# Recurrence order, row halves, and attention scores inside the last recurrent round, with GpSimd scaling the rows

## The chip, the cores and the metric

The kernel runs on one core of one Trainium2 chip. The metric is the device time of one execution in microseconds; the runs of the kernel before gave 2823.59 to 2827.82 us with a median of 2827.42. The engines of the core are TensorE (matrix products, with its weight loads), VectorE, ScalarE, GpSimd and SyncE, which issues transfers.

## The reference

Two transformer blocks on 256 positions of width 2048, in float32. The first block is normed, projected by w_in, and its columns are shared between two mixers. Then follow an output projection, a cross attention to a memory, and an MLP; the second block is a gated chunk mixer and a convolutional feed-forward with modulation from `ada_w`. The change lies in the two mixers of the first block.

The first mixer is a recurrence over 16 heads of 64 (RWKV-7):

```python
w = -jax.nn.softplus(-(w0 + jnp.tanh(xw) @ w_decay_up)) - 0.5
decay = jnp.exp(-jnp.exp(w.astype(f32)))
a = jax.nn.sigmoid(a0 + xa @ a_up)
g = jax.nn.sigmoid(xg) @ g_up
kk = heads(k * k_k); kk = kk / jnp.maximum(jnp.sqrt(jnp.sum(kk * kk, axis=-1, keepdims=True)), 1e-12)
k = k * (1.0 + (a - 1.0) * k_a)
def step(state, inp):
    r_t, w_t, k_t, v_t, kk_t, a_t = inp
    sa = jnp.einsum('bhvk,bhk->bhv', state, -kk_t)
    state = (state * w_t[:, :, None, :] + sa[..., None] * (kk_t * a_t)[:, :, None, :]
             + v_t[..., None] * k_t[:, :, None, :])
    return state, jnp.einsum('bhvk,bhk->bhv', state, r_t)
# ... y is normed per head, (yn + bonus) * g, bonus = sum(r k r_k) v
```

The second mixer is sparse attention with 8 query heads and 2 key heads of 128. An index score (16 heads of 64, relu, weighted sum) picks 64 of the causal keys for each query; the kernel turns the choice into a bias of 0 or -1e30 and does an ordinary softmax:

```python
s = jnp.einsum('bqhgd,bqkhd->bqhgk', qg, kg) * (ATT_HEAD ** -0.5)
prob = jax.nn.softmax(jnp.where(valid, s, -inf), axis=-1)
o = jnp.einsum('bqhgk,bqkhd->bqhgd', prob, vg)
```

## The kernel before, in words

The sequence is 256 positions (T), kept as two blocks (b = 0, 1) of 128 rows or four chunks of 64 columns. Each engine's instructions are written out in one order by hand; an engine does them in that order. Waits are on counters: `Steps` gives each step of a list a name, `done` counts it up when the instruction ends, and `wait(engine, lane, round, name)` makes the engine wait until that step has been counted. The lists (PD, PA, PT for the preparation, CD, CA, CT for the core of the recurrence, YD, YA, YT for its tail, HD, HA, HT for the attention, the last letter for VectorE, ScalarE or TensorE) must hold the steps in the order in which they are done.

**Recurrence.** It is done in four rounds (i = 0 to 3) of two lanes (g = 0, 1), each lane a tile of two heads. Within a chunk the recurrence is the inverse of a triangular matrix, found by doubling: for level lv = 1 to 5 TensorE multiplies (`product`, step p), ScalarE copies the product out of PSUM (c), TensorE squares and multiplies (`doubled`, step q), and VectorE merges the results by a masked copy into `xx` (x for one half, z for the other; line 787). Then TensorE applies the inverse (`applied`: au, ry, mn), VectorE forms the carried sums (`state`: r2 on line 795, mt, nn on line 804, st on line 809, with the products s1 and s2 of line 1101 in between) and TensorE the outputs (yy, line 1109). The tail norms them (`mean`, `variance`, `inverse`, `normed`, `low_part`).

The tiles of round i + 1 are prepared between the levels of round i. On TensorE: the head norms (line 930) and the decay and gain LoRA products (`lora_t`, lines 939 and 940) ahead of the first doubling, the gate (lines 947 and 948) ahead of the second, the spread norm (line 953) ahead of the third, the bonus product (`bonus_t`, line 968) ahead of the fifth. The LoRA weights of decay and gain have 64 rows each that are not zero. On VectorE: norm km after level 1, inverse after 2, key after 3, decay sum and bonus input bp after 4, bonus bo (line 740) and the decayed tiles of both lanes (`decayed_d`: at on line 747, b0 on line 750, bk on line 751, rt on line 753) after 5, ahead of `state`. TensorE turns the decayed tiles (`turn_t`, lines 979 to 983): lane 0 between s1 and s2, lane 1 after yy. In the last round nothing is prepared.

**Attention.** The index scores (`index_tensor`, line 625) and the choice of keys are made within the projection; the bias is ready at 288 us. At the end of the last round TensorE makes the score products of heads 0 to 3 (line 1137). After `low_part(3)` VectorE takes for head k the score out of PSUM with scale and bias (sm, line 903), two row maxima (ma, mb) and their negative (ng); ScalarE does the exponentials with row sums (line 458); VectorE takes the reciprocal (rc) and scales the rows (na, nb, lines 912 and 913); TensorE turns the three 128x128 squares (line 1148), ScalarE copies them (pc, line 465), TensorE multiplies with the values (lines 1205 to 1207) and makes the scores of head k + 4, and the result is split in a high part (h, line 470) and a low part (lo, line 917). Four tiles `sm` serve eight heads in turn. All engines wait for the last HD step before the output projection; SyncE fetches its first four blocks and ScalarE the memory tensor when the recurrence's tail is done. GpSimd has nothing to do from 288 us to 538 us.

## Time and profile before

| what | value |
|---|---|
| median of 3 runs | 2827.42 us |
| profiled execution, its own time | 2827.2 us |
| span | 2825.4 us |
| instructions | 49020 |
| TensorE busy | 2725.5 us (96%) |
| VectorE busy | 2024.3 us (72%) |
| ScalarE busy | 1395.1 us (49%) |
| GpSimd busy | 173.7 us (6%) |
| mean granted TensorE clock | 0.981 |
| recurrence, first chunk product to last low part | 333.14 to 500.70 us |
| attention, to its last low part | 500.70 to 523.28 us |

The span is the time from the first to the last instruction of the profiled execution. Busy times count an engine's instructions, not its waits. Matrix products are pipelined, so a busy TensorE is not one at its peak. The granted clock is a share of 2.4 GHz: 1.00 is 2.4 GHz and 0.50 is 1.2 GHz. A float32 product shows as two records. In the timelines a row is a run of alike instructions: its start, its length, the engine, the line and the tiles (written<-read), how many, and in brackets the idle time before it and what ended that.

### The profile page before, as it was taken

What the parts mean: (1) busy time and instruction counts of PE and PEld (TensorE: products, weight loads), DVE (VectorE), ACT (ScalarE), POOL (GpSimd) and SP (SyncE); (2) the same over time, 40 slices, a digit from 0 to 9 for tenths busy, and PEclk for the clock granted to TensorE, in tenths of its full rate; (3) what the DMA queues carried; (4) which work ended last, traced back from release to release, by engine and by line L of the source; (5) the groups of instructions that cost most, each with busy time, mean ns of one, the idle gap of its engine ahead of it and who ended that gap; (6) DMA issues with size and microseconds to landing.
All of it is one profiled execution on the core that took longest, in us unless ns stands there. A gap on an engine that the chain in (4) does not pass through costs nothing.

```text
span 2825.4 us, 49020 instructions
## 1 busy us (share of the span) xinstructions
PE 2725.5 (96%) x17934; PEld 2335.7 (83%) x17934; DVE 2024.3 (72%) x3189; ACT 1395.1 (49%) x2215; POOL 173.7 (6%) x211
## 2 busy tenths in 40 slices
PE   9999988799899999999999999999999999999997
PEld 8877777687688888888876888888878888888886
DVE  5566566686788887878888766668787656775675
ACT  5444454555544444444445454445465545554554
POOL 4500000210100000000030000000100000000002
PEclk9999999899999999999999999999999999999999
DMA  6554200454477777887767865567745555555553
GB/s 213 173 170 153 98 3 3 160 176 149 163 284 281 276 285 263 292 292 269 276 238 264 295 243 167 180 239 283 260 157 185 191 190 186 181 190 187 181 186 135
DMA packets 157712, 573.35 MB, mean 203 GB/s; under 512 B 17984, under 2 KB 18272, under 8 KB 157120
## 3 DMA queue, kind: packets, MB, share of 16 engines
q1 hardware_dynamic: 154368, 562.11, 58.0%
q10 hardware_dynamic: 2064, 7.50, 0.7%
q8 instruction: 141, 2.31, 0.3%
q0 software_dynamic: 1072, 0.89, 0.2%
q14 instruction: 67, 0.55, 0.1%
HBM read 567.57 MB, written 2.10 MB: 202 GB/s over the span
## 4 chain that ended last, share of the span: by engine, by line
PE 84%; DVE 9%; POOL 3%; issue 2%; ACT 2%; DMA 0%; POOLq 0%; DVEq 0%; ACTq 0%
PE ps L2298 45%; PE ps L2299 24%; DVE wlo L1978 3%; PE ps L2301 3%; PE ps L2323 2%; PE ps L2325 2%; PE ps L2324 2%; DVE tt L2063 1%; POOL tab L288 1%; PE ps L1646 1%; DVE tt L2005 1%; POOL ssm L1734 0%; PE ps L1035 0%; ACT whi L1755 0%; DVE xn L2052 0%
## 5 line engine op out<-in xcount | busy, mean ns | idle before, releaser
L1978 DVE TENSOR_TENSOR wlo<-raw,whi 128x1024 fp32r<-128x1024 f32 x872 | 1061.5, 1230 | 399.2 <-ACT whi L1755 397.7
L2298 PE MATMUL ps<-xn,whi 128*128 128x512 f32 x3540 | 1261.8, 401 | 12.5 <-issue 5.1
L1755 ACT ACTIVATE whi<-raw 128x1024 fp32r<-128x1024 f32 x872 | 907.1, 1054 | 586.1 <-PE ps L2299 516.9
L2299 PE MATMUL ps<-xn,wlo 128*128 128x256 f32 x3776 | 1053.6, 282 | 0.0
L2298 PE MATMUL ps<-act_in,whi 128*128 128x512 f32 x2444 | 871.5, 401 | 7.5 <-issue 3.4
L2298 PEld LDWEIGHTS ps<-xn,whi 128*128 128x128 f32 x3540 | 669.3, 189 | 178.7 <-issue 11.0
L2299 PE MATMUL ps<-act_in,wlo 128*128 128x256 f32 x2624 | 732.0, 282 | 0.0
L2299 PEld LDWEIGHTS ps<-xn,wlo 128*128 128x128 f32 x3776 | 717.6, 190 | 5.1
L2298 PEld LDWEIGHTS ps<-act_in,whi 128*128 128x128 f32 x2444 | 462.5, 189 | 122.1 <-DVE wlo L1978 4.8
L2299 PEld LDWEIGHTS ps<-act_in,wlo 128*128 128x128 f32 x2624 | 498.8, 190 | 4.0
L1762 ACT ACTIVATE hl<-ps 128x256 f32<-128x256 f32 x416 | 155.4, 375 | 354.9 <-PE ps L2301 354.9
L2005 DVE TENSOR_TENSOR tt<-ps,hl 128x256 f32<-128x256 f32 x272 | 113.6, 418 | 161.0 <-ACT hl L1762 159.3
L1732 POOL COPY ss<-tt 128x256 f32<-128x256 f32 x5 | 2.6, 527 | 1955.2 <-ACT tt L1793 1955.2
L1804 ACT ACTIVATE act_in<-tt 128x256 fp32r<-128x256 f32 x140 | 56.6, 418 | 123.7 <-DVE tt L2160 88.7
L2323 PE MATMUL ps<-whi,xn 128*128 128x512 f32 x288 | 112.6, 391 | 3.8 <-issue 1.8
L2325 PE MATMUL ps<-whi,xn 128*128 128x512 f32 x288 | 112.2, 389 | 0.0
L2324 PE MATMUL ps<-wlo,xn 128*128 128x512 f32 x288 | 112.1, 389 | 0.0
L1998 DVE SCALAR_TENSOR_TENSOR ada<-adaq,silu_c,ada 128x512 f32<-128x512 f32 (+1 forms) x128 | 100.5, 785 | 2.3
L1998 DVE SCALAR_TENSOR_TENSOR ada<-adaw,silu_c,ada 128x512 f32<-128x512 f32 (+1 forms) x112 | 83.9, 749 | 2.4
L2301 PE MATMUL ps<-xn,whi 128*128 128x512 f32 x236 | 85.0, 394 | 0.0
L1734 POOL TENSOR_TENSOR ss<-ss,tt 128x256 f32<-128x256 f32 x75 | 67.7, 903 | 217.5 <-ACT tt L1793 214.5
L2005 DVE TENSOR_TENSOR zc<-ps,hl 128x256 f32<-128x256 f32 x88 | 37.0, 420 | 56.0 <-ACT hl L1762 56.0
(329 smaller groups left out, 2095.5 us busy)
## 6 DMA issues: line engine op xcount, KB each, us to landing
raw<-in_stream SPq DMA_DIRECT2D x872, 512.0 KB, 4.2
adaw<-in_ada SPq DMA_DIRECT2D x96, 512.0 KB, 5.6
adaq<-in_ada SPq DMA_DIRECT2D x96, 512.0 KB, 4.9
h<-in_xT SPq DMA_DIRECT2D x4, 512.0 KB, 7.6
memx<-in_memT ACTq DMA_DIRECT2D x1, 2048.0 KB, 9.3
out<-fin SPq DMA_DIRECT2D x4, 512.0 KB, 2.6
lwa<-in_lora ACTq DMA_DIRECT2D x1, 1536.0 KB, 8.2
wst<-in_wsT ACTq DMA_DIRECT2D x1, 1024.0 KB, 4.8
```

What stands on the lines that cost most here:

```text
L1734: pool.tensor_tensor(acc[:, :], acc[:, :], new, ALU.add).then_inc(ss_done, 1)
L1755: act.activation(whi[:, r, :], raw[:, r, :], ACT.Copy).then_inc(hi_done, 1)
L1762: act.activation(hl[:, t, :], ps[:, lin.bank(g, t), T:2 * T], ACT.Copy).then_inc(hl_done, 1)
L1978: dve.tensor_tensor(wlo[:, r, :], raw[:, r, :], whi[:, r, :].bitcast(F32), ALU.subtract)\
L1998: ins = dve.scalar_tensor_tensor(dst, w, s, dst, ALU.mult, ALU.add)
L2005: dve.tensor_tensor(dst, ps[:, lin.bank(g, t), 0:T], hl[:, t, :], ALU.add).then_inc(evac_done, 1)
L2298: pe.matmul(ps[:, b, :], whi[:, r, w], x[:, kc, :], start=first, stop=False)
L2299: ins = pe.matmul(ps[:, b, 0:T], wlo[:, r, w], x[:, kc, 0:T], start=False, stop=False)
L2301: ins = pe.matmul(ps[:, b, :], whi[:, r, w], x[:, kc, :], start=False, stop=True)
L2323: pe.matmul(out, hi, whi[:, r, w], start=first, stop=False)
L2324: pe.matmul(out, hi, wlo[:, r, w], start=False, stop=False)
L2325: ins = pe.matmul(out, lo, whi[:, r, w], start=False, stop=last)
```

## The change

1. VectorE's masked copies of a level do x of both lanes first and then z of both (before: x and z of lane 0, then of lane 1).
2. The bonus product of the next round stands after the last doubling on TensorE, not before it.
3. `decayed_d` is split in two (at and b0; `grown_d`: bk and rt). Lane 0's stay ahead of `state`; lane 1's stand inside it, the first half ahead of s2 and the second ahead of s3.
4. The LoRA products read only the 64 rows of their part, and each part has its own bank (decay in one, gain in the other, the lanes side by side); ScalarE reads them there. In the index scores the loops over heads and blocks are swapped, so that products of the upper and the lower 64 rows alternate.
5. In the last round the scores of heads 0 to 3 are made behind the doublings of levels 1 to 4, VectorE does their maxima behind its copies of these levels, and ScalarE their exponentials ahead of its copies for levels 3, 4 and 5 and ahead of `applied`. At the end of the round TensorE makes the scores of heads 4 to 7, and in the attention none.
6. There are eight tiles `sm`. GpSimd scales the rows, each head after its reciprocal. VectorE's loop is reciprocal k, maxima k + 4, low part k - 2; ScalarE's is exponentials k + 4, copy k, high part k - 1.

```diff
@@ level copies, bonus product, decays
         def doubled(i, lv):
-            for g in lanes:
-                CT.wait(dve, g, i, f"q{lv}")
-                for w in range(2) if lv < 5 else (1,):
+            for w in range(2) if lv < 5 else (1,):
+                for g in lanes:
+                    if w == 0 or lv == 5:
+                        CT.wait(dve, g, i, f"q{lv}")
...
             product(i, 5)
+            doubled(i, 5)
             if more:
                 bonus_t(pe, i + 1)
-            doubled(i, 5)
             applied(i)
...
             for c in (1, 2):
+                if i < 3:
+                    (decayed_d, grown_d)[c - 1](dve, i + 1, (1,))
                 for g in lanes:
...
                 bonus_v_d(dve, i + 1)
-                decayed_d(dve, i + 1)
+                decayed_d(dve, i + 1, (0,))
+                grown_d(dve, i + 1, (0,))
             state(i)
@@ row halves
+        for g in lanes:
+            n, o = 2 * i + g, slice(g * T, (g + 1) * T)
+            for k in range(2):
+                r = rows(k)
+                ins = pe.matmul(bank(i, k, "wa")[:, o], lwa(n, k)[r, :], lora_in(0)[r, :], start=True, stop=True)
+            PT.done(ins, g, "wa")
...
-            for hd in range(2):
-                q = slice(CH * hd, CH * hd + CH)
-                for b in range(2):
+            for b in range(2):
+                for hd in range(2):
+                    q = slice(CH * hd, CH * hd + CH)
@@ last round: TensorE (lv 1 to 4), ScalarE (k = 0 to 3), VectorE (k = 0 to 3)
             doubled(i, 1)
+            if not more:
+                scores(0)
             product(i, 2)
...
                 root_k_a(act, i + 1)
+            else:
+                exponentials(0)
             product(i, 3)
...
                 norm_k_d(dve, i + 1)
+            else:
+                JP.wait(dve, 0, 0, "d1")
+                maxima(0)
             doubled(i, 2)
...
                 if i < 3:
                     PD.wait(pe, g, i + 1, "bo")
+                else:
+                    HD.wait(pe, 0, 0, f"sm{2 + g}")
@@ attention: GpSimd, then VectorE
+        for k in range(8):
+            HD.wait(pool, 0, 0, f"rc{k}")
+            for b, name in enumerate("ab"):
+                v = sm[k][:, 0:P] if b == 0 else sm[k][:, P:384]
+                HP.done(pool.tensor_scalar(v, v, sx_[:, k, 2 + b:3 + b], None, ALU.mult), 0, f"n{name}{k}")
...
+        for k in range(10):
             if k < 8:
+                HA.wait(dve, 0, 0, f"eb{k}")
+                hd_(f"rc{k}", dve.reciprocal(sx_[:, k, 2:4], sx_[:, k, 2:4]))
+            if k < 4:
+                maxima(k + 4)
+            if k >= 2:
+                q = k - 2
                 HA.wait(dve, 0, 0, f"h{q}")
...
         def turned_p(k):
-            HD.wait(pe, 0, 0, f"nb{k}")
+            HP.wait(pe, 0, 0, f"nb{k}")
```

## Rows read from the trace of the kernel before

**Rows 1.** The page's chain that ended last: shares of the span by engine.
```profile
PE 84%; DVE 9%; POOL 3%; issue 2%; ACT 2%; DMA 0%; POOLq 0%; DVEq 0%; ACTq 0%
```

**Rows 2.** Windows: stretch, busy by engine (records), TensorE clock, DMA share, GB/s.
```profile
333.14:500.70 167.56, 142.84 (x3669) 121.34 (x3668) 103.91 (x314) 77.12 (x182) 0.00 (x0) 0.94 0.04 12
500.70:523.28 22.58, 14.66 (x88) 12.40 (x88) 18.30 (x65) 15.66 (x50) 0.00 (x0) 0.77 0.47 186
411.00:420.00 9.00, 7.96 (x64) 6.66 (x66) 3.21 (x13) 3.36 (x8) 0.00 (x0) 0.62 0.01 2
447.00:450.00 3.00, 3.00 (x47) 3.00 (x48) 1.44 (x4) 0.00 (x0) 0.00 (x0) 0.52 0.02 5
```

**Rows 3.** Chain of waits, second round: start us, us, what ran.
```profile
402.63 0.49 DVE bp L734
405.44 0.64 DVE bo L740 x2
409.68 0.67 DVE r L795 x2
411.68 0.48 DVE nn L804 x2
```

**Rows 4.** Timeline of VectorE, first and third round, between the state products.
```profile
373.75 0.48 DVE L809 SCALAR_TENSOR_TENSOR st<-ps,e,nn 128x64 f32<-128x64 f32 x2 [1.00 <-PE ps L1101]
...
458.72 0.50 DVE L809 SCALAR_TENSOR_TENSOR st<-ps,e,nn 128x64 f32<-128x64 f32 x2 [1.85 <-PE ps L1101]
```

**Rows 5.** Timeline of VectorE, last round: levels, then state.
```profile
473.30 1.44 DVE L787 COPY_PREDICATED xx<-mk,ps 128x256 f32<-128x256 int32 x4 [0.34 <-PE ps L1049]
475.74 1.43 DVE L787 COPY_PREDICATED xx<-mk,ps 128x256 f32<-128x256 int32 x4 [1.00 <-PE ps L1049]
...
480.59 0.44 DVE L787 COPY_PREDICATED xx<-mk,ps 128x256 f32<-128x256 int32 x1 [0.94 <-PE ps L1049]
...
487.31 0.66 DVE L804 TENSOR_SCALAR nn<-ps,e 128x64 f32<-128x64 f32 x3
```

**Rows 6.** Timeline of TensorE: LoRA products of two rounds, then one index score.
```profile
343.69 0.91 PE L939 MATMUL ps<-proj,lwa 128*128 128x256 f32 x2 [1.40 <-DMA lwa<-in_lora]
...
427.97 0.68 PE L939 MATMUL ps<-proj,lwa 128*128 128x256 f32 x2
...
429.35 0.59 PE L940 MATMUL ps<-proj,lwa 128*128 128x256 f32 x2
...
125.08 0.93 PE L625 MATMUL ps<-ki,proj 64*128 64x128 f32 x8
```

**Rows 7.** Line 625 alone, from 125.10 to 125.11: records running then.
```profile
L625 PE MATMUL ps<-ki,proj x2: 373/373/373, 125.1 to 125.1; 64*128 64x128 f32 x2
```

**Rows 8.** Timeline of VectorE in the attention: first two heads, then the end.
```profile
500.62 0.55 DVE L903 SCALAR_TENSOR_TENSOR sm<-ps,bias 128x384 f32<-128x384 f32 x1
501.93 0.55 DVE L903 SCALAR_TENSOR_TENSOR sm<-ps,bias 128x384 f32<-128x384 f32 x1
...
519.93 0.34 DVE L913 TENSOR_SCALAR sm<-sm,sx__211 128x256 f32<-128x256 f32 x1
...
522.85 0.42 DVE L917 TENSOR_TENSOR act_in<-ps,act_in 128x256 fp32r<-128x256 f32 x1 [0.42 <-ACT act_in L470]
```

**Rows 9.** Timeline of TensorE: the attention's first product.
```profile
504.40 0.90 PE L1148 MATMUL ps<-ident,sm 128*128 128x128 f32 x3 [7.44 <-DVE sm L913]
```

**Rows 10.** Timeline of GpSimd in the projection: two products of a table by a constant.
```profile
61.73 1.92 POOL L288 TENSOR_SCALAR tab<-tp 128x256 f32<-128x256 f32 x1
...
97.61 0.85 POOL L288 TENSOR_SCALAR tab<-tp 128x256 f32<-128x256 f32 x1
```

**Rows 11.** Timeline of VectorE beside the first of these.
```profile
61.71 1.23 DVE L1978 TENSOR_TENSOR wlo<-raw,whi 128x1024 fp32r<-128x1024 f32 x1 [1.61 <-ACT whi L1755]
```

**Rows 12.** Timeline of ScalarE after the attention: a table load and its activation.
```profile
567.26 1.28 ACT L1773 ACT_TABLE_LOAD   x1
568.87 0.42 ACT L1773 ACTIVATE nx<-nx 128x256 f32<-128x256 f32 x1 [0.32 <-DVE nx L2029]
```

More of the change, by code:

```diff
@@ L418, in high, with exponentials @@
                 YA.done(act.activation(act_in[:, 2 * i + g, 0:T], yq[g][:, :], ACT.Copy), g, "hi")
+        def exponentials(k):
+            HD.wait(act, 0, 0, f"ng{k}")
+            for b in range(2):
+                v = sm[k][:, 0:P] if b == 0 else sm[k][:, P:384]
+                HA.done(act.activation(v, v, ACT.Exp, bias=sx_[:, k, b:b + 1], accum_out=sx_[:, k, 2 + b:3 + b]),
+                        0, f"e{'ab'[b]}{k}")
         unit(0)
@@ L441, in scalar @@
                 decays_a(act, i + 1)
+            else:
+                exponentials(3)
             applied(i)
@@ L740, in bonus_v_d, with decayed_d @@
             pd(dve, i, g, "bo", dve.tensor_tensor(bo[2 * (i % 2) + g][:, :], bank(i, g, "bs")[:, 0:T], tiles(2 * i + g)[2], ALU.mult))
-    def decayed_d(dve, i):
-        for g in lanes:
+    def decayed_d(dve, i, which=lanes):
+        for g in which:
             q = 2 * (i % 2) + g
@@ L749, in decayed_d, with grown_d @@
             pd(dve, i, g, "at", ins)
-            pd(dve, i, g, "b0", dve.tensor_tensor(tb[i][g][:, 0, :], kk[i][g][:, :], aa[i][g][:, :], ALU.mult), True)
+            pd(dve, i, g, "b0", dve.tensor_tensor(tb[i][g][:, 0, :], kk[i][g][:, :], aa[i][g][:, :], ALU.mult))
+    def grown_d(dve, i, which=lanes):
+        for g in which:
+            q = 2 * (i % 2) + g
+            PD.wait(dve, g, i, "b0")
             pd(dve, i, g, "bk", dve.tensor_tensor(bk[q][:, :, :], tb[i][g][:, :, :], e2[i][g][:, :].unsqueeze(1).to_broadcast([P, 2, T]),
@@ L851, in low_part, with hd_, maxima @@
                                                   ALU.subtract))
+        def hd_(name, ins, chain=False):
+            HD.done(ins, 0, name)
+            if chain:
+                HD.wait(dve, 0, 0, name)
+        def maxima(k):
+            HT.wait(dve, 0, 0, f"s{k}")
+            hd_(f"sm{k}", dve.scalar_tensor_tensor(sm[k][:, :], ps[:, (2, 6, 3, 7)[k % 4], 0:384], ATT_SCALE, bias[:, :],
+                                                   ALU.mult, ALU.add), True)
+            hd_(f"ma{k}", dve.tensor_reduce(sx_[:, k, 0:1], sm[k][:, 0:P], AX_X, ALU.max))
+            hd_(f"mb{k}", dve.tensor_reduce(sx_[:, k, 1:2], sm[k][:, P:384], AX_X, ALU.max), True)
+            hd_(f"ng{k}", dve.tensor_scalar(sx_[:, k, 0:2], sx_[:, k, 0:2], -1.0, None, ALU.mult))
         for g in lanes:
@@ L865, in vector @@
                 inverse_k_d(dve, i + 1)
+            else:
+                maxima(1)
             doubled(i, 3)
@@ L868, in vector @@
                 key_d(dve, i + 1)
+            else:
+                maxima(2)
             doubled(i, 4)
@@ L872, in vector @@
                 bonus_d(dve, i + 1)
+            else:
+                maxima(3)
             doubled(i, 5)
@@ L966, in bonus_t @@
             PD.wait(pe, g, i, "bp")
-            PA.wait(pe, g, i, "aa")
+            for z in lanes:
+                PA.wait(pe, z, i, "aa")
             PT.done(pe.matmul(bank(i, g, "bs")[:, 0:T], blk[:, 0, :], bp[i][g][:, :], start=True, stop=True), g, "bs")
@@ L1131, in scores @@
             if k < 2:
[L1132 to L1135 removed]
+                CA.wait(pe, k, 3, "zw")
+            elif k < 4:
+                YD.wait(pe, k - 2, 2, "yn")
+            else:
+                CA.wait(pe, k % 2, 3, "y1")
+                CD.wait(pe, k % 2, 3, "n2")
             for b in range(2):
@@ L1168, in tensor @@
             doubled(i, 2)
+            if not more:
+                scores(1)
             product(i, 3)
@@ L1172, in tensor @@
             doubled(i, 3)
+            if not more:
+                scores(2)
             product(i, 4)
             doubled(i, 4)
+            if not more:
+                scores(3)
             product(i, 5)
+            doubled(i, 5)
             if more:
                 bonus_t(pe, i + 1)
-            doubled(i, 5)
             applied(i)
@@ L1182, in tensor @@
             else:
-                for k in range(4):
+                for k in range(4, 8):
                     scores(k)
```

91 lines of the change are left out of this document (29 added, 62 removed).

## The prediction

> **What bounds the kernel now.** I read the chain of waits first, then the windows by stage, then the timelines of the engines in the stages that the change touches. TensorE holds 84% of the chain that ended last [rows 1], and nearly all of that lies in the weight streams, which the change leaves alone. What it touches is the recurrence (333.14 to 500.70 us, 167.6 us) and the attention behind it (500.70 to 523.28 us, 22.6 us) [rows 2]. No engine is full there: TensorE is busy 142.8 us of the first and 14.7 of the second, VectorE 103.9 and 18.3. The work goes back and forth between the engines in small pieces, so an order that lets a piece start earlier moves the end. In the attention VectorE, 81% busy, is closest to a bound. The stage behind starts when all attention steps are counted, so what is won or lost here moves the rest of the program as a whole. The four weight blocks and the memory tensor, 4.2 MB, land within the attention (186 GB/s over 22.58 us [rows 2]); in 19 us they would need 220, which the page's slices show to be common (up to 295), so they stay hidden.
>
> **The change part by part.** Everything is set against the profiled execution, 2827.2 us with a span of 2825.4; that is 0.2 us below the median of the runs, so the difference carries over. A time within 0.2% (5.7 us) of it is what a measurement can't tell from no change.
>
> *Bonus product behind the last doubling, and lane 1's decays later.* In the second round the bonus input bp is ready at 403.12 us. Then came bonus product, doubling, x5 and bo (up to 406.08), 3.6 us of decays for two lanes, the state's first sum at 409.68, and the three products nn of lane 1, done at 412.16 [rows 3]: 9.0 us. With the new order the last doubling is done while VectorE still makes bp, and x5 follows bp at once. From there the path is what the last round shows, where VectorE has no decays to make: from the end of lane 0's x5 (481.03) to the end of nn (487.97) [rows 5], 6.94 us. Add 0.44 for that x5 and 0.22 for the later end of VectorE's copies (below): 7.6 us, 1.4 saved. VectorE's bo and lane 0's decays (0.7 + 1.8 us) fit beside TensorE's and ScalarE's steps, with 0.3 to spare. This counts in three rounds: -4.2. In the third TensorE was granted 0.52 of its clock (the 1.2 GHz level) from 447 to 450 us [rows 2], inside this path, and the new order has the idle time before it cut by the doubling; half of the 1.4 us that this costs, -0.6, is counted. Bounds: 0 to -2.5 a round.
>
> *Where lane 1's decays go.* They now stand between the state products: 0.86 us ahead of s2 and 1.0 ahead of s3, in front of both lanes' steps. In the first round VectorE sat idle there for 1.00 us, in the third for 1.85 [rows 4], since TensorE's transposes, at 1.2 GHz in the second and third round, took longer. So 1.86 us don't fit in the first (+0.9) and do in the two others (0). If TensorE keeps its clock in those two, it is +0.9 each, but then the transposes and chunk products win more.
>
> *Order of the copies.* x of both lanes, then z of both. The second x must wait for lane 1's doubling, so VectorE ends about 0.2 us later, and lane 1's next product starts up to 0.15 earlier. Where VectorE goes on to something urgent (km before the gate product, bp) it costs 0.2; elsewhere nothing. The 0.2 is in the sums here.
>
> *Row halves.* The LoRA products run over 64 rows each, decay on the upper and gain on the lower half, into two banks. Before, four 128-row products took from 427.97 to 429.9 us [rows 6], about 0.46 each, on TensorE's path. If halves run side by side two pairs take 0.9: 0.9 saved, less 0.2 for another tile shape and 0.2 for km: -0.5 a round. That different tiles do run together the index scores show: 10 ns after their first record started, two are running [rows 7]. In the first round these products run slower (0.91 for the first pair of records against 0.68 [rows 6]): -1.1. The product pair in the projection, where TensorE is the bound: -0.5. Together -2.6, bounds 0 and -4.4. The Trainium skill ("TensorEngine Tiling (Array Packing)", Key Properties) says that a change of tiling mode drains the engine; by it each LoRA block pays a drain on both sides, where before it paid one, and this is a rule against the edit. No row has this very switch. In the index scores the same edit is only a swap of loops: as two records already run together, it brings 0; if those two are halves of one product, 0.2 x 8 = -1.6 at most, kept for the range.
>
> *Last round: scores and maxima inside.* Four score products (384 columns each; the index score of as many took 0.93 us [rows 6]) lie beside VectorE's copies and cost nothing. VectorE's maxima of one head take 1.31 us (500.62 to 501.93 [rows 8]) and stand in front of the next level's copies. Its idle time there is 1.00 us a level [rows 5]. So VectorE becomes the bound: free at 472.96, level 2 starts at 474.27 instead of 473.30; each further level is 1.36 + 1.31 = 2.67 instead of 2.44; x5 starts at 482.28 instead of 480.59: +1.7. The exponentials lie in ScalarE's idle time (it is busy 77 of 168 us [rows 2]). They need a table load of 1.28 us, but a load ran ahead of the wait of its activation (567.26, the activation then still waited 0.32 [rows 12]), so it lies beside VectorE's work. The Sqrt table comes back after the state and is hidden by the scores of heads 4 to 7. If the load is not hidden it is +1; low bound +0.8, high +3.
>
> *Attention.* VectorE loses four maxima (5.2 us) and all scalings (0.34 us for the larger half of a head [rows 8]); GpSimd gets the scalings. A 128x256 product by one constant took it 0.85 us [rows 10]; for 128x128 I take 0.5, with the gap 1.45 a head (bounds 1.3 and 3.0). Nothing can start before VectorE has the last low part and the first reciprocal, so heads 0 to 3 still pass GpSimd one after the other. First head, in us from the start: reciprocal 0.3, GpSimd done at 1.8, transposes 0.9 ([rows 9]: TensorE is at its lower clock after the idle time, as before) to 2.8, copy 3.3, next head's transposes, product to 5.5, high part 6.0, low part 6.45. VectorE's order puts the reciprocal of head 3 behind that low part, and the one of head k behind the low part of k - 3. Such a round is 5.9 us (the tail below plus 1.2 of queueing): head 6 at 12.3, head 7 behind the next low part at 14.7. The tail from a head's scaling to the end was 523.28 - 520.27 = 3.0 [rows 8]; with GpSimd 1.65 it ends at 19.4. Before: 22.6. So -3.2; low bound GpSimd alone in a row, 0.3 + 8 x 1.45 + 3.1 = 15.0 (-7.6), high bound below.
>
> *Sum:* rounds -4.2 - 0.6 + 0.9; LoRA -2.6; last round +1.7; attention -3.2: -8.0. 2827.2 - 8.0 = 2819.
>
> **Rivals.**
> *A. TensorE's clock holds through (faster).* From 411 to 420 us it was granted 0.62 [rows 2]; that stretch cost 9 x 0.38 = 3.4 us at most. With shorter idle times the drops in the second and third round may go: -4, and 0.9 back for the decays in each: some 2 to 4 more, 2816. For it: the new order closes TensorE's idle times. Against: attention starts with TensorE idle for over 5 us all the same.
> *B. GpSimd is slowed by VectorE (no change).* The same product by a constant took 1.92 us when a VectorE operation ran beside it (61.71, 1.23 us, both inputs in SBUF) [rows 10, 11]. At this rate a head costs 3.0 us: 0.3 + 8 x 3.0 + 3.1 = 27.4, 4.8 more than before, which eats the rest of the gain: 2827. Against: VectorE's big operations in the attention read one input from PSUM. The Trainium skill ("SBUF — State Buffer", SBUF: two separate sides) has GpSimd block only against VectorE operations with two SBUF inputs or in a two-port mode; by that rule this rival falls.
> *C. The pairs don't pair and the loop through VectorE is longer (same).* LoRA 0, attention -1.5, last round +2.5: about -3, 2824.
> *D. The clock drops more often (slower).* The drops follow short idle times between dense stretches. If all four rounds get one like 411 to 420, where two had it in part, it adds 4 x 3.4 = 13.6 less some 3 that is already there: +10.6, 2830. It outweighs the gain from the third such stretch on. For it: round one's waits on VectorE at s3 grow; against: everything else fills idle time.
>
> **How the numbers follow.** My forecast 0.54 (its own range 2815 to 2823), A 0.12, B 0.12, C 0.13, D 0.09. Faster by over 0.2% (below 2821.7): nine tenths of the first and all of A, 0.61. Slower by over 0.2% (above 2833) only the worse half of D: 0.05. The rest, 0.34, is within 0.2%. The range reaches to A with a shorter attention below (2812) and to B and most of D above (2829).
>
> **What would show it.** Right: bp to nn about 7.6 us in the second round; VectorE's x5 right behind bp; LoRA block 1 us instead of 1.9; levels of the last round 2.7 us apart, bound by VectorE; GpSimd 1.4 to 1.5 us a head and the attention 19 to 20 us. Wrong: GpSimd over 2 us a head; a table load between ng and c3 in the last round that holds up TensorE; a TensorE clock below 1 in new places; index scores shorter than 0.87 us.

## The result: 2812.3 us, 12 to 16 us faster, with most of it in the recurrent rounds

| | before | after |
|---|---|---|
| median of five runs each | 2824.42 us (2821.69 to 2827.82) | 2812.34 us (2810.79 to 2813.57) |
| ratio | | 0.9942, 95% interval 0.9928 to 0.9957 |
| profiled execution, its own time | 2827.2 us | 2812.44 us |
| span | 2825.4 us | 2810.6 us |
| first chunk product to last low part | 167.6 us | 155.7 us |
| attention | 22.6 us | 19.8 us |
| behind the attention | 2302.1 us | 2302.2 us |

The prediction was 2819, that is -8. The measured difference is -16 us by the ratio of all runs (-12 to -20), -14.8 us by the spans of the two profiled executions, and -12.1 us by the two medians; the five runs of the kernel before scatter by 6 us. So it went the way that was forecast, and one and a half times to twice as far.

Windows of the kernel after (stretch, busy of each engine with its records, TensorE clock, DMA share, GB/s). The first two and the last two answer to [rows 2]; the others split the second round at the end of lane 1's bonus input bp, the end of the last sum nn and the first copies of the next round.

```profile
332.93:488.60 155.67, 135.19 (x3685) 115.13 (x3684) 109.52 (x330) 83.80 (x200) 0.00 (x0) 0.98 0.05 13
488.60:508.38 19.78, 13.48 (x72) 11.92 (x72) 9.05 (x33) 11.82 (x34) 12.02 (x16) 0.70 0.53 212
399.08:405.97 6.89, 5.94 (x198) 5.05 (x198) 5.80 (x21) 3.76 (x8) 0.00 (x0) 1.00 0.01 2
405.97:415.73 9.76, 9.06 (x210) 8.01 (x210) 6.91 (x23) 5.17 (x14) 0.00 (x0) 1.00 0.01 3
411.00:420.00 9.00, 9.00 (x232) 8.10 (x232) 7.66 (x20) 5.14 (x15) 0.00 (x0) 1.00 0.02 5
447.00:450.00 3.00, 3.00 (x54) 2.60 (x56) 1.27 (x4) 1.85 (x5) 0.00 (x0) 1.00 0.02 5
```

The same parts of the kernel before, first to third round:

```profile
372.03:381.41 9.38, 9.06 (x210) 8.02 (x210) 5.42 (x17) 5.28 (x15) 0.00 (x0) 1.00 0.02 4
403.11:412.14 9.03, 7.08 (x230) 6.06 (x230) 7.49 (x27) 3.90 (x9) 0.00 (x0) 1.00 0.01 2
412.14:424.36 12.22, 11.99 (x210) 10.61 (x210) 5.44 (x18) 5.29 (x15) 0.00 (x0) 0.72 0.01 3
446.06:456.15 10.09, 8.18 (x230) 7.19 (x230) 7.50 (x27) 3.90 (x9) 0.00 (x0) 0.83 0.01 3
456.15:466.82 10.67, 10.44 (x210) 9.18 (x210) 5.43 (x16) 4.49 (x13) 0.00 (x0) 0.84 0.01 2
```

Two things are to be seen. First, bp to nn went from 9.03 to 6.89 us at full clock. Second, the stretch from nn to the next copies holds the same work in each round (210 records), and takes 9.38 us at full clock but 12.22 and 10.67 where the clock fell to its 1.2 GHz level for a time. After the change it takes 9.76 in each round, the clock is 1.00, and the two stretches that stood at 0.62 and 0.52 before stand at 1.00. (At the start of the first round, from about 342 to 348 us, the clock is below 1.00 in every kernel; that stretch isn't counted as a fall here.)

VectorE's timeline of the kernel after, second round (answers to [rows 3]):

```profile
398.60 0.48 DVE L749 SCALAR_TENSOR_TENSOR bp<-proj,par,tb 128x256 f32<-128x256 f32 x1
399.00 0.77 DVE L808 COPY_PREDICATED xx<-mk,ps 128x256 f32<-128x256 int32 x2
...
401.79 0.42 DVE L773 TENSOR_TENSOR ar<-proj,e 128x256 f32<-128x256 f32 x1
402.55 0.42 DVE L816 TENSOR_TENSOR r<-ps,ar 128x256 f32<-128x256 f32 x1 [0.34 <-PE ps L1111]
403.42 0.42 DVE L816 TENSOR_TENSOR r<-ps,ar 128x256 f32<-128x256 f32 x1 [0.45 <-PE ps L1111]
...
405.31 0.66 DVE L825 TENSOR_SCALAR nn<-ps,e 128x64 f32<-128x64 f32 x3
```

x5 of both lanes follows bp at once, and lane 0's decayed tiles are done 0.34 us before the first sum can start.

The whole difference of the spans, part by part ("fall" is a time behind 348 us in which TensorE's clock was below 1.00):

| part | predicted | measured |
|---|---|---|
| bp to nn, three rounds at full clock | -4.2 | 9.04 to 6.79, 6.89, 6.82: -6.6 |
| falls of the clock in the three rounds | -0.6 | 10.09 - 9.03, 12.22 - 9.38, 10.67 - 9.38 are gone: -5.2 |
| lane 1's decays between the state products | +0.9 | 9.38 to 9.76, three times: +1.1 |
| first copies of a round to bp (LoRA halves, order of the copies) | -2.1 | -1.3, -0.7, -0.7: -2.6 |
| products in the projection | -0.5 | first chunk product 333.14 to 332.93: -0.2 |
| last round | +1.7 | +1.4 |
| attention | -3.2 | -2.8 |
| behind it | 0 | +0.1 |
| sum | -8.0 | -14.8 |

These are one execution of each kernel, and two rows aren't clean. The first chunk product starts anywhere from 330.1 to 333.2 us in the other profiled executions, with the projection written either way, so -0.2 is no measurement. The -1.3 of the first round holds a wait for the LoRA weights' transfer; that part took 22.1 to 24.1 us over the executions of kernels with the row halves (e13, e10).

### The profile page after: what moved, and what is told of

The parts are those of the page before. It is cut to its first block, busy times and chain, and to the rows that moved or that the text cites. A ratio compares the mean times of both kernels' runs of the same rounds, so it can differ in the third digit from the quotient of the medians.

```text
span 2810.6 us, 49025 instructions
## 1 busy us (share of the span) xinstructions
PE 2715.5 (97%) x17934; PEld 2328.1 (83%) x17934; DVE 2020.7 (72%) x3173; ACT 1398.7 (50%) x2217; POOL 186.5 (7%) x227
## 4 chain that ended last, share of the span: by engine, by line
PE 87%; DVE 8%; issue 2%; ACT 2%; POOL 1%; DMA 0%; POOLq 0%; DVEq 0%; ACTq 0%
PE ps L2341 47%; PE ps L2342 25%; PE ps L2344 3%; DVE wlo L2021 3%; PE ps L2366 2%; PE ps L2368 2%; PE ps L2367 2%; PE ps L1689 1%; DVE tt L2048 1%; ACT whi L1798 0%; POOL ssm L1777 0%; DVE tt L2106 0%; PE ps L1068 0%; PE ps L1081 0%; PE ps L2414 0%
```

## Experiments

Twelve kernels were timed, each with runs of the kernel before beside it on the same chip. The kernel before spread from 2821.7 to 2838.4 us over all of them; each ratio is against the runs beside it. A thirteenth, e6, was to fill TensorE's idle time ahead of the attention. It gave no time, so what the clock costs there has no run of its own (more on it below).

### Which half of the change brings it

**Recurrence alone (e1).** The kernel before with edits 1 to 4.

> The kernel before with edits 1 to 4 of the change (order of the copies, bonus product, decays, row halves) and the attention as before. Clock theory: the traces show 13.3 us less from the first product of the first round to that of the last, so this kernel alone takes 13 to 15 us less than before, with a granted TensorE clock of 1.00 in all 3 us stretches from 351 us to the end of the recurrence; the last round is 0.5 us shorter. Rival (the scores inside the last round and the attention carry the gain): 6 us less or under. As predicted blind the four edits were worth 8 us less 1.7 and 3.2 for the rest, 6.5.

**Attention alone (e2).** The kernel before with edits 5 and 6.

> The kernel before with edits 5 and 6 (scores, maxima and exponentials of four heads in the last round, eight tiles, GpSimd scaling) and the recurrence's old order. By the traces of the change: last round +1.4, attention -2.8, so -1 to -2 us. If the two groups of edits lean on each other (the last round with the old copy order is longer, the clock lower), between 0 and +2.

Measured: e1 2814.0 us, ratio 0.9944 (0.9926 to 0.9961), its clock 1.00 from 348 to 483 us; e2 2824.3 us, 0.9986 (0.9972 to 0.9999). The gain lies in the recurrence. The attention edits are worth -1.4 us by the table (+1.4 and -2.8). e2 agrees but can't measure it: its ratio allows -0.3 to -7.9, and its falls aren't those of the kernel before.

### Is it the clock?

**Idle time filled (e3).** The kernel before, its order untouched; TensorE makes products that nobody reads where it would wait.

```diff
             if more:
+                filler(3, 3)
                 bonus_t(pe, i + 1)
             doubled(i, 5)
@@ state products
+            if i < 3:
+                CA.wait(pe, 0, i, "y1")
+                filler(2, 2)
             for c in (1, 2):
@@
+        def filler(n, bank):
+            for _ in range(n):
+                mm(ps[:, bank, T:2 * T], blk[:, 0, :], lora_in(0), start=True, stop=True)
```

> The kernel before, with products that nobody reads put in TensorE's idle time of rounds 1 to 3: three ahead of the bonus product and two ahead of s1 (each 128x256, 0.43 us). No dependency gets shorter. Clock theory: TensorE is granted 1.00 from 405 to 465 us where before it had 0.50 to 0.72 (411 to 420), 0.52 (447 to 450) and 0.62 to 0.82 (456 to 462); the second and third round end 5.2 us sooner less up to 0.5 a round for products that reach past the wait: 3.5 to 5 us less than before. Rival (the clock is only a sign, the dependencies are what counts): 0 to 2 us more than before.

Measured: 2821.9 us, 0.9973 (0.9963 to 0.9983), so -7.6 us (-4.8 to -10.5) for work that only adds; by the spans of the profiled executions it is -4.9, which is what was expected. Windows of e3, and the stretch from nn to the next copies in its third round:

```profile
348.00:480.00 132.00, 124.00 (x3328) 104.76 (x3324) 88.27 (x269) 68.86 (x162) 0.00 (x0) 1.00 0.01 3
450.84:460.21 9.37, 9.05 (x209) 8.01 (x209) 5.41 (x16) 4.48 (x13) 0.00 (x0) 1.00 0.02 3
```

That stretch is 9.37 us where the kernel before took 10.67, and bp to nn stays at 9.04: the order is as slow as it was, only the falls are gone (one came in the last round instead, 482 to 486 us). This is the mechanism of rival A, shown without any of the edits.

**Bonus product's order alone (e4), and all but it (e5).** e4 is the kernel before with `doubled(i, 5)` ahead of `bonus_t`; e5 is the changed kernel with the two swapped back.

```diff
             product(i, 5)
+            doubled(i, 5)
             if more:
                 bonus_t(pe, i + 1)
-            doubled(i, 5)
```

> The kernel before with edit 2 alone (the bonus product behind the last doubling). Between bp and the decays 1.4 us a round go (bonus product and doubling out of the chain), but both lanes' decays, 3.6 us, stay ahead of the state's sums. My theory: 3 x 1.4 = 4.2 us from this path; the idle time before the bonus product falls from 1.65 to 0.7 us but the one before s1 stays, so the clock may still drop at s1: 4 to 5 us less without a change of the clock, 9 if it holds everywhere.

> The changed kernel with edit 2 undone: the bonus product is ahead of the last doubling again, with 1.65 us of idle TensorE in front of it. Order theory: 1.5 to 2 us more a round in three rounds, 4.5 to 6 us more than the changed kernel, so 9 to 11 us less than before. Clock theory on top: one or two stretches of the recurrence fall to 1.2 GHz again, each 1 to 3 us; in sum 5 to 10 us more than the changed kernel.

Measured: e4 2820.1 us, 0.9965 (0.9953 to 0.9976); e5 2817.6 us, 0.9956 (0.9941 to 0.9972). Windows of e4 (bp to nn in the second round, nn to the next copies in the third), then of e5 (bp to nn, second and third round):

```profile
401.67:409.07 7.40, 5.94 (x198) 5.05 (x198) 7.29 (x26) 3.90 (x9) 0.00 (x0) 1.00 0.01 2
447.55:459.76 12.21, 11.99 (x210) 10.22 (x210) 5.49 (x16) 4.49 (x13) 0.00 (x0) 0.72 0.01 1
```

```profile
400.27:409.58 9.31, 8.31 (x230) 7.57 (x230) 6.00 (x22) 3.75 (x7) 0.00 (x0) 0.82 0.01 2
440.36:448.38 8.02, 6.86 (x230) 5.96 (x230) 5.93 (x22) 3.76 (x7) 0.00 (x0) 1.00 0.02 4
```

On the path the order alone takes 1.64 us of the 9.04 away in each round, the decays alone 1.02, both together 2.2. But neither alone ends the falls: e4 still has two in the three rounds, e5 one. The totals fit loosely: e4's three times 1.64 are 4.9 us, its span is 4.2 below that of the kernel before, and its ratio says 9.9.

**Decays back (e9), and the same with idle time filled (e13).** e9 is the changed kernel with all eight decayed tiles ahead of the state:

```diff
             for c in (1, 2):
-                if i < 3:
-                    (decayed_d, grown_d)[c - 1](dve, i + 1, (1,))
...
-                decayed_d(dve, i + 1, (0,))
-                grown_d(dve, i + 1, (0,))
+                for z in lanes:
+                    decayed_d(dve, i + 1, (z,))
+                    grown_d(dve, i + 1, (z,))
```

> The changed kernel with the first half of edit 3 undone: lane 1's decayed tiles are made ahead of the state again, all eight in front of its first sum; everything else as changed. Path theory: VectorE had 0.3 us to spare ahead of the first sum, so lane 1's 1.86 us come back on the path between bp and nn, about +1.5 in each of three rounds, and the way from s1 to yy gives 0.37 back: the rounds go from 39.9, 37.7, 37.6 us to about 41.0, 38.8, 38.7, in all +3.4 us, with TensorE's clock at 1.00 throughout. Rival 1 (only the order of the bonus product matters, the decays hide behind TensorE's last doubling): within 0.5 us of the changed kernel. Rival 2 (the longer idle time of TensorE ahead of s1 lets its clock fall in at least one round): +5 us or more, and a stretch below 0.9 between 348 and 480 us.

e13 adds to e9 the fillers of e3, two ahead of the bonus product and two ahead of s1.

> The kernel of e9 (all eight decayed tiles ahead of the state) with TensorE's idle time filled: two unread 128x256 products ahead of the bonus product and two ahead of s1 in rounds one to three. It asks whether the 5.8 us that e9's span was longer than the changed kernel's are the path or the clock. Clock theory: of e9's length only 0.52 - 0.37 = 0.15 us a round is path; the two stretches from nn to the next round's first copies that took 12.29 us at a low clock go back to 9.4, TensorE's clock is 1.00 from 348 to 477, and the span is 2811 to 2812, the median within 0.7 us of the changed kernel's 2812.3. Rival (path: the decays ahead of the state cost what they take, and the low clock is a by-product): the span stays at 2815 or more even where the clock is full, bp to nn in 8 us or more.

Measured: e9 2815.2 us (2812.1 to 2818.2), 0.9943 (0.9924 to 0.9962), its span 5.8 us over that of the changed kernel. e13 2810.5 us (2809.1 to 2812.6), 0.9929 (0.9914 to 0.9943), its span 2810.2. Windows of e9 (nn to copies, first round; bp to nn and nn to copies, second; nn to copies, third), then of e13 (bp to nn and nn to copies, second round; and 126 us of the rounds):

```profile
367.43:379.72 12.29, 12.02 (x210) 10.43 (x210) 5.47 (x16) 5.29 (x15) 0.00 (x0) 0.72 0.02 3
400.74:408.15 7.41, 5.84 (x198) 5.04 (x198) 7.30 (x27) 3.58 (x8) 0.00 (x0) 1.00 0.01 2
408.15:417.53 9.38, 9.06 (x210) 8.01 (x210) 5.42 (x17) 5.29 (x15) 0.00 (x0) 1.00 0.01 3
445.96:458.25 12.29, 12.04 (x210) 10.45 (x210) 5.48 (x16) 4.50 (x13) 0.00 (x0) 0.72 0.01 3
```

```profile
397.19:404.60 7.41, 6.96 (x202) 5.81 (x202) 7.30 (x27) 3.58 (x8) 0.00 (x0) 1.00 0.02 4
404.60:413.97 9.37, 9.05 (x209) 8.00 (x209) 5.41 (x16) 5.29 (x15) 0.00 (x0) 1.00 0.01 2
348.00:474.00 126.00, 119.04 (x3318) 101.28 (x3316) 94.14 (x285) 74.13 (x176) 0.00 (x0) 1.00 0.01 4
```

The first expectation of e9 (+3.4 by the path) failed: on the path the late decays save 0.52 to 0.62 us between bp and nn and give 0.38 back behind it, 0.14 to 0.24 a round. Its second rival held: there are two falls, of 2.91 us each. e13 has e9's path within 0.02 us and no falls in these rounds, and is as fast as the changed kernel. So nearly all that edit 3 is worth in this kernel, it is worth through TensorE's clock. What shows it are the stretches (12.29 against 9.37 and 9.38 us). The totals alone would not: e9's profiled execution was the slowest of its four, its median is only 2.9 us above that of the changed kernel, and its ratio is the same (0.9943 and 0.9942). The equal spans of e13 and the changed kernel hold some chance too: e13 is 2.1 us earlier at the end of the first round's bp, and loses 1.5 to a fall in the last round.

TensorE's time without work between bp and nn in the first round, where every kernel has the full clock (length less busy time), and how many of the first three rounds of the profiled execution have a fall:

| kernel | idle, us | of three rounds, with a fall | spread of its runs, us |
|---|---|---|---|
| before | 2.2 | 2 | 2821.7 to 2838.4 |
| e11 (below) | 2.2 | 2 | 2820.7 to 2833.7 |
| e4 | 1.7 | 2 | 2815.3 to 2824.5 |
| e9 | 1.7 | 2 | 2812.1 to 2818.2 |
| e5 | 1.2 | 1 | 2815.7 to 2819.9 |
| e3 | 1.1 | 0 | 2816.8 to 2824.1 |
| after | 1.1 | 0 | 2810.8 to 2813.6 |
| e10 (below) | 1.1 | 0 | 2809.6 to 2812.7 |
| e13 | 0.6 | 0 | 2809.1 to 2812.6 |

Falls go with idle time here, but the idle time of this stretch alone doesn't set them: e5 and e3 are within 0.1 us of each other, and one has a fall. Why e9's second round has none with nearly the same idle time as its first (1.6 and 1.7 us) is open.

The kernels with falls in the trace scatter more from run to run, mostly, which fits falls that come and go. That is weak evidence: it was only seen on totals, one execution of each was profiled, and the kernels that scatter more were mostly run more often (e3, e4 and e11 10 to 12 times, the others 4 to 6). e3 scatters too, though its trace has none in the three rounds.

The last round isn't in the table. Seven of the kernels have a fall of about 4 us there, behind its sums nn, between 475 and 487 us: e3, e5, e7, e9, e10, e12 and e13. In e9, e10 and e13 that round, up to its last low part, is 1.4 to 1.9 us longer than in the changed kernel, which has none there. So an edit that ends the falls of three rounds doesn't always end them in the fourth.

### The small terms

**Order of the copies (e10).** The changed kernel with x and z of one lane together again.

```diff
-            for w in range(2) if lv < 5 else (1,):
-                for g in lanes:
-                    if w == 0 or lv == 5:
-                        CT.wait(dve, g, i, f"q{lv}")
+            for g in lanes:
+                CT.wait(dve, g, i, f"q{lv}")
+                for w in range(2) if lv < 5 else (1,):
```

> The changed kernel with edit 1 undone (x and z of lane 0, then x and z of lane 1). Theory from the two traces: with the new order the second lane's x comes 0.2 us earlier at each level and x5 of the lanes 0.36 instead of 1.0 us apart, so undoing it costs 0.15 to 0.2 us at each of four levels in four rounds and up to 0.5 more where x5 is waited for in three: +2 to +4 us. Rival, the working of the prediction (the later end of VectorE's copies costs 0.2 where something urgent follows, elsewhere nothing): undoing it gains 0.2 to 1 us. If the clock falls somewhere that it didn't, 1 to 3 us come on top.

Measured: 2811.5 us, 0.9932 (0.9913 to 0.9950), span 2810.8. Levels 2 to 4 of the second round, e10 and then the kernel after:

```profile
387.15 1.43 DVE L807 COPY_PREDICATED xx<-mk,ps 128x256 f32<-128x256 int32 x4 [2.68 <-PE ps L1081]
390.71 1.44 DVE L807 COPY_PREDICATED xx<-mk,ps 128x256 f32<-128x256 int32 x4 [1.99 <-PE ps L1081]
393.39 1.43 DVE L807 COPY_PREDICATED xx<-mk,ps 128x256 f32<-128x256 int32 x4 [0.48 <-PE ps L1081]
```

```profile
388.60 1.57 DVE L808 COPY_PREDICATED xx<-mk,ps 128x256 f32<-128x256 int32 x4 [2.68 <-PE ps L1082]
392.08 1.57 DVE L808 COPY_PREDICATED xx<-mk,ps 128x256 f32<-128x256 int32 x4 [1.78 <-PE ps L1082]
394.66 1.57 DVE L808 COPY_PREDICATED xx<-mk,ps 128x256 f32<-128x256 int32 x4 [0.24 <-PE ps L1082]
```

With the new order the copies of a level take 0.14 us longer in all, and the next ones start 0.1 us sooner after them (3.48 and 2.58 us apart instead of 3.56 and 2.68). From the first copies to bp it is 21.03 us after and 20.95 in e10. My theory of +2 to +4 us, made from the two traces, was wrong: in these rounds edit 1 does next to nothing, as the prediction's working had it. The total says no more, since e10 has a fall in its last round that the changed kernel lacks. The 0.36 us between the lanes' x5 comes from the bonus product's order.

**LoRA halves alone (e11).**

```diff
-            pe.matmul(bank(i, g, "wa")[:, 0:T], lwa(n, 0), lora_in(0), start=True, stop=True)
-            PT.done(pe.matmul(bank(i, g, "wa")[:, T:2 * T], lwa(n, 1), lora_in(0), start=True, stop=True), g, "wa")
+            for k in range(2):
+                r = rows(k)
+                ins = pe.matmul(bank(i, k, "wa")[:, o], lwa(n, k)[r, :], lora_in(0)[r, :], start=True, stop=True)
+            PT.done(ins, g, "wa")
```

> The kernel before with the LoRA half of edit 4 alone. Pairing theory: the block of four products goes from 1.97 to about 1.15 us in the rounds at full clock and from 3.5 to about 1.9 in the first, so the rounds' prepared tiles come 0.8 us earlier; the gate product waits for km 0.3 longer, and the total falls by 1.5 to 3.5 us. Rival 1 (off the path: TensorE waits for km all the same): the block is shorter, the total within 0.5 us. Rival 2 (TensorE's clock still falls, since its idle times ahead of the bonus product and of s1 stay): the falls stay near 411 to 420 and 444 to 460 us and rounds two and three stay above 41 us. If the halves don't pair, the block stays at 1.9 us or more.

Measured: 2827.5 us, 0.9997 (0.9985 to 1.0009). The block in its second round, and the stretch from bp to nn behind it:

```profile
383.76 1.13 PE L942 MATMUL ps<-proj,lwa 64*128 64x256 f32 x8
```

```profile
401.02:410.76 9.74, 8.46 (x230) 7.58 (x230) 7.49 (x26) 3.89 (x9) 0.00 (x0) 0.82 0.01 2
```

The block is short, and from the first copies to bp the round takes 20.95 us instead of 21.70, so the 0.75 us are real on the path. In the total they can't be told from nothing: the falls are still there, and they scatter by more than the 2.8 us that three rounds should bring.

### The attention

**VectorE scales the rows (e8)** in the changed kernel, each head right behind its reciprocal:

```diff
-        for k in range(8):
-            HD.wait(pool, 0, 0, f"rc{k}")
-            ... pool.tensor_scalar(v, v, sx_[:, k, 2 + b:3 + b], None, ALU.mult)
+                for b, name in enumerate("ab"):
+                    hd_(f"n{name}{k}", dve.tensor_scalar(v, v, sx_[:, k, 2 + b:3 + b], None, ALU.mult))
```

> The changed kernel with the row scaling back on VectorE (0.29 and 0.35 us a head), in the same loop order. My theory: the scaling's 1.5 us on GpSimd is a leg of the loop from reciprocal to low part, VectorE has the room (busy under 45% of the attention), so 0.7 us a head for six heads go: 2 to 5 us less than the changed kernel. Rival (GpSimd's help is what made the attention shorter): 1 to 3 us more.

**First four heads finished early (e7)**: their reciprocals stand ahead of the last state, so that GpSimd scales them within the last round; the maxima of heads 4 and 5 stand in the tail, ahead of the last low part, those of 6 and 7 right behind it, and two heads are turned and copied ahead of the last low part. **e12** is e7 with VectorE scaling heads 4 to 7.

```diff
@@ e7, VectorE: ahead of the last state; in the tail and behind it
+            else:
+                for k in range(4):
+                    inverted(k)
             state(i)
...
+            if i == 3:
+                maxima(4)
...
+        maxima(5)
         low_part(3)
+        maxima(6)
+        maxima(7)
@@ e7, ScalarE: behind variance(3)
+        preload(act, ACT.Exp)
+        exponentials(4)
+        copied(0)
+        copied(1)
         high(3)
@@ e12
-        for k in range(8):
+        for k in range(4):
             HD.wait(pool, 0, 0, f"rc{k}")
```

> A version meant to beat both. The changed kernel with more of the attention inside the recurrence's last round: reciprocals 0 to 3 ahead of the last state, so GpSimd scales heads 0 to 3 beside the tail; one score product instead of four ahead of the last mean, the others behind mean and inverse; maxima of head 4 inside the tail; exponentials of head 4 and the first two copies ahead of the last high part; low parts no longer ahead of maxima. The tail is 2 us shorter (three scores of 0.72 us leave the chain, less what they cost later) and the attention 19.8 -> 12 to 15 us: 6 to 9 us less than the changed kernel. If the loop of pc, o, h, lo through two buffers sets the attention (2.0 us a head as now), only 3 to 4 us less.

> Meant to beat the others: the version whose first four heads are finished inside the last round (e7), with VectorE scaling the rows of heads 4 to 7 and GpSimd only those of heads 0 to 3. In e7 GpSimd's chain of four heads sets the pace at 1.48 us a head, from 491.93 to 497.87 us, and the last low part ends at 500.87. VectorE takes 0.15 + 0.2 wait + 0.55 a head, TensorE's transposes and products with ScalarE's copy and high part about 1.1 to 1.2 us a head: the last low part ends 1.2 to 2 us earlier, about 499.2, and the total is 2802 to 2803. Rival (the stage behind is late for its weights: a block landed at 508.34 after 3.5 us of waiting): the attention ends earlier, the total stays at 2804.

Measured: e8 2810.0 us, 0.9935 (0.9915 to 0.9954); e7 2804.0 us, 0.9909 (0.9889 to 0.9928); e12 2805.4 us, 0.9910 (0.9892 to 0.9929). e8 is 2.3 us below the changed kernel by the medians, less than the two kernels scatter, so its gain rests on the trace. e7 beats both kernels, the changed one by 8.3 us by the medians and 6.8 by the spans (2803.8 us). The attention takes 16.8 us in e8, 11.7 in e7 and 10.5 in e12, against 19.8. The tail of the recurrence isn't the 2 us shorter that I expected of e7: it ends at 489.2 us, where the changed kernel's ends at 488.6, with a fall of the clock from 477 to 481 in it. GpSimd on heads 4 to 7 in e7, then windows behind the attention in e7 and in e12:

```profile
491.93 5.94 POOL L314 TENSOR_SCALAR sm<-sm,sx__215 128x128 f32<-128x128 f32 x8 [15.78 <-DVE sx__215 L888]
```

```profile
501.00:504.00 3.00, 0.62 (x3) 0.60 (x4) 1.95 (x2) 3.00 (x4) 0.00 (x0) 1.00 0.02 10
504.00:507.00 3.00, 3.00 (x13) 2.57 (x12) 2.69 (x3) 0.80 (x1) 0.00 (x0) 0.62 0.77 235
```

```profile
501.00:504.00 3.00, 2.39 (x7) 2.13 (x8) 3.00 (x4) 2.02 (x3) 0.00 (x0) 0.50 0.46 132
504.00:507.00 3.00, 3.00 (x11) 2.52 (x11) 0.92 (x1) 0.00 (x0) 0.00 (x0) 0.50 0.93 305
```

e12's attention is 1.3 us shorter, as expected to the lower side, and the total is not. I had put a late weight block as the rival. A part of it is another one: the output projection starts 1.77 us earlier than in e7, but with TensorE at 0.50 for its first 5.7 us, where e7 began at 1.00 and was at 0.50 from 505 to 508 us. At its tenth product of 512 columns e12 is 0.7 us ahead. ScalarE's fifth block of weights waited for TensorE (4.15 us) in e12, for its transfer (3.54 us) in e7. The spans end 0.2 us apart; where the rest went is open.

**The clock in the attention.** In the changed kernel TensorE stands at 0.50 from 487 to 500.7 us, for the first 12 us of the attention. e2, e9 and e13 have the same attention, and in them the clock is back after 6.6 to 7.5 us. Theirs takes 18.75 us, not 19.8. e9's:

```profile
494.92:513.67 18.75, 11.84 (x72) 10.19 (x72) 8.99 (x33) 11.77 (x34) 11.97 (x16) 0.81 0.56 224
```

So the clock is worth about 1 us there between such cases. In e8 too it was back after 8.4 us, so of the 3.0 us by which e8's attention is shorter, up to 1 may be the clock's, and 2 the scaling's. What an attention wholly at full clock would take wasn't measured.

## Why the prediction was right in sign and short in size

**The step that failed is the clock's, predicted at -0.6 us and measured at -5.2** ("half of the 1.4 us that this costs, -0.6, is counted", and rival A's "some 2 to 4 more" at a chance of 0.12). The kernel before lost 5.2 us to falls in its three rounds: 2.8 in the stretch that [rows 2] show at 0.62, 1.1 in the one at 0.52, 1.3 behind it (456 to 462 us), for which I had taken no row. All of it went. The trace of before had this in it: the stretch from nn to the next copies is 9.38 us in the first round and 12.22 in the second for the same 210 records, and nothing but the clock differs between them. I compared the rounds only where the edits touched them, and but for the -0.6 gave the falls to the change as a chance, not as a term. e3 shows the mechanism without an edit of the order, e13 that it carries nearly all of edit 3. This is 4.6 of the 6.8 us that the sum is short. Another 2.4 are the next paragraph's, and the other rows come to 0.2 the other way.

**bp to nn: right in place, 0.8 us short in each round.** Where 7.6 us were predicted, 6.8 to 6.9 came. The stand-in, the last round of before, has x5 of the two lanes 1.0 us apart, because there it waits for TensorE; behind bp both are ready, and run 0.36 apart. The 0.22 for the later end of the copies wasn't paid either, since bp and not the copies came last. The bonus product's order carries 1.64 of the 2.2 us (e4).

**Lane 1's decays: the sum right (+1.1 for +0.9) by luck.** I had them at +0.9 in the first round and at nothing in the others, from TensorE's slow transposes there; with the clock held, the same working would have given +2.7. With the clock at 1.00 the rounds are alike, and each pays 0.38. The error is in the first round as well. The 0.75 us ahead of s2 are paid in full. But from there to the next sum it then takes 1.32 us where it took 1.69, so the half ahead of s3 costs nothing and 0.37 comes back.

**Order of the copies: right**, nothing but 0.08 us a round (e10, second and third round).

**Row halves: right in the rounds, wrong in the projection.** TensorE's timeline of the kernel after: the LoRA products of the first and second round, the gate products of the third, and the index score that answers to [rows 6]:

```profile
343.31 1.85 PE L971 MATMUL ps<-proj,lwa 64*128 64x256 f32 x8 [1.21 <-DMA lwa<-in_lora]
381.74 1.13 PE L971 MATMUL ps<-proj,lwa 64*128 64x256 f32 x8
423.59 0.70 PE L979 MATMUL ps<-proj,lwa 128*128 128x256 f32 x2 [0.70 <-DVE rk L724]
125.93 0.93 PE L640 MATMUL ps<-ki,proj 64*128 64x128 f32 x8
```

The block fell from 1.97 to 1.13 us, and the gate products then waited 0.70 us for km. So the halves pair. The Trainium skill ("TensorEngine Tiling (Array Packing)", Key Properties) has a change of tiling mode drain the engine. No row shows such a drain by itself. From the block's first product to the first doubling product behind it, both changes of shape included, it is 1.06 us where it was 1.91, so the edit is worth it. The index scores stayed at 0.93 us, so the swap of loops is worth nothing. That the two records of [rows 7] were two products is shown by the kernel before itself:

```profile
L625 PE MATMUL ps<-ki,proj x4: 272/322/373, 125.1 to 125.3; 64*128 64x128 f32 x4
```

These four records, all that run up to 125.33 us, are those of the two products with 128 columns, one of each row half. In the program a product with 256 columns stands between the two, and its records start later. So the two halves already ran side by side. The product in the projection was put at -0.5; what it brought is lost in the scatter of the first chunk product's start.

**Last round: right in sum (+1.4 for +1.7), partly by luck.** VectorE's copies and ScalarE's table load in the kernel after:

```profile
460.69 1.43 DVE L808 COPY_PREDICATED xx<-mk,ps 128x256 f32<-128x256 int32 x4
463.32 1.43 DVE L808 COPY_PREDICATED xx<-mk,ps 128x256 f32<-128x256 int32 x4
466.22 1.57 DVE L808 COPY_PREDICATED xx<-mk,ps 128x256 f32<-128x256 int32 x4 [0.17 <-PE ps L1082]
469.29 0.91 DVE L808 COPY_PREDICATED xx<-mk,ps 128x256 f32<-128x256 int32 x2 [0.21 <-PE ps L1082]
```

```profile
459.66 1.28 ACT L429 ACT_TABLE_LOAD   x1
460.95 0.40 ACT L429 ACTIVATE sm<-sm,sx__215 128x128 f32<-128x128 f32 x1
```

The levels are 2.63, 2.90 and 3.07 us apart where 2.67 was said: VectorE bounds the first, and then TensorE, which makes a score of 0.92 us between doubling and product, is 0.17 to 0.21 us later than VectorE. With the first step (457.39 to 460.69) x5 starts 2.2 us later in the round than before, not 1.7. A term that I had left out gives 0.8 of it back: the copies of x5 of the two lanes now follow each other at once, and from their start to the end of nn it is 6.61 us where it was 7.38. The table load ran while VectorE was still at the maxima (their last step ended at 460.78), so it was hidden but for 0.2 us.

**Attention: right within 0.4 us, at the clock that it met.** GpSimd, TensorE's first product and VectorE's last low part, kernel after (answer to [rows 8, 9]):

```profile
488.81 4.48 POOL L315 TENSOR_SCALAR sm<-sm,sx__215 128x128 f32<-128x128 f32 x6 [201.33 <-DVE sx__215 L940]
495.26 1.51 POOL L315 TENSOR_SCALAR sm<-sm,sx__215 128x128 f32<-128x128 f32 x2 [1.97 <-DVE sx__215 L940]
...
503.87 1.51 POOL L315 TENSOR_SCALAR sm<-sm,sx__215 128x128 f32<-128x128 f32 x2 [0.50 <-DVE sx__215 L940]
```

```profile
490.38 0.90 PE L1185 MATMUL ps<-ident,sm 128*128 128x128 f32 x3 [5.50 <-POOL sm L315]
```

```profile
507.95 0.42 DVE L946 TENSOR_TENSOR act_in<-ps,act_in 128x256 fp32r<-128x256 f32 x1 [0.42 <-ACT act_in L485]
```

GpSimd takes 1.5 us a head for the 1.45 said. The loop through the low part was seen as well: GpSimd sits idle 1.97 us for the fourth reciprocal. What I didn't draw from it is that the hand-over to GpSimd doesn't pay: VectorE, which then waits for up to 2.4 us at a time, does the two scalings in 0.55 us, and the attention is 2 to 3 us shorter with it (e8). Rival B fell: a head takes 1.49 us beside VectorE's maxima and 1.51 without them. Rival D came in none of the changed kernel's rounds ahead of the last tail. Rival A was the mechanism, and its 2 to 4 us more were still too few.

## What to carry to other kernels

Cut the rounds of a loop at the same steps and compare the lengths of the parts. Where the same records take longer in one round and the clock is below 1.00 there, the loss is a term of its own, and an edit that takes out idle time ahead of that part may win all of it, though a fall may then turn up in a later part. Unread products in TensorE's idle time are a cheap test of that, and here they were a gain by themselves (0.9973). Judge an edit of 1 or 2 us by the like parts of two traces and not by the totals, where it drowns. When a step is handed to an idle engine, compare its duration with the time in which the first engine waits anyway.

## What the runs showed of the hardware

- TensorE's clock fell though it was busy for most of the time before: in e9 it was busy 5.71, 5.84 and 5.75 us of 7.4 from bp to nn in the three rounds, and behind the first and the third came a fall that cost 2.9 us, behind the second none.
- A fall can turn up elsewhere: with the idle time of the rounds filled, e3 and e13 have one in the last round (482 to 486 and 475 to 479 us) that the kernels before and after don't have there.
- The same attention took 19.8 us with TensorE at 0.50 for its first 12 us, and 18.75 with 6.6 to 7.5 us of that (e2, e9, e13).
- Products on the upper and the lower 64 rows ran side by side though the program had another product between them (125.08 to 125.33 us, kernel before).
- GpSimd's product by one number for each row took 0.60 us for 128x128 and 0.92 us for 128x256 float32; VectorE's two took 0.55 us together.
- A table load for the exponentials (459.66 us, 1.28 us long) ran while the activation behind it still lacked VectorE's last maxima step (ended at 460.78).
